# Two transformer blocks on one core: the moving columns of the main products in another order

## The reference

```
# block 1
z = rmsnorm(x) @ w_in                       # 2048 -> 5200
... pooling mixer, top-k attention ...
x = x + concat(y_pool, y_attn) @ w_out      # 2048 -> 2048
up = rmsnorm(x) @ w_up                      # 2048 -> 11264
x = x + (silu(conv(gate)) * conv(val)) @ w_down    # 5632 -> 2048
# block 2
proj = rmsnorm(h) @ w_in_2                  # 2048 -> 8000
... two attentions; w_uq_2, w_ukv_2, w_branch_a_2, w_branch_b_2 ...
h = h + mixed @ w_out_2                     # 2048 -> 2048
h = h + (silu(hn @ w_gate_2) * (hn @ w_up_2)) @ w_down_2   # 2048 -> 2 x 5632 -> 2048
return rmsnorm(h)
```

## Time and profile before

| | |
|---|---|
| median of 3 executions | 2428.22 us (2427.38 to 2428.86) |
| the profiled execution: time | 2428.58 us |
| its span, first to last instruction | 2426.7 us |
| PE busy | 2417.1 us, 11684 matmuls |
| PEld busy | 2036.5 us, 11684 loads |
| DVE, ACT, POOL busy | 1371.2, 1178.5, 59.8 us |
| transfers | 449.40 MB, mean 185 GB/s |
| granted TensorE clock, mean | 0.999 |

### The profile page before, as it was taken

The page is one execution under the profiler, slowest core; times in us unless marked ns, Lnnn a source line. Parts: engine busy times, 40 slices in busy tenths (PEclk is TensorE's granted clock), DMA queues, the critical chain, the costliest instruction groups (busy, mean ns, idle before and its releaser), DMA issues.

```text
span 2426.7 us, 31051 instructions
## 1 busy us (share of the span) xinstructions
PE 2417.1 (100%) x11684; PEld 2036.5 (84%) x11684; DVE 1371.2 (57%) x1594; ACT 1178.5 (49%) x1534; POOL 59.8 (2%) x100
## 2 busy tenths in 40 slices
PE   9999999999999999999999999999999999999998
PEld 8788888888888888888888888888888888888887
DVE  5675456777777765445454454665545445454544
ACT  5544445555555544445455544544444444444443
POOL 0000000000000000001120000000000000000000
PEclk9999999999999999999999999999999999999999
DMA  7665456666666655556655556556666666666664
GB/s 249 176 178 167 148 183 182 192 186 185 192 192 179 195 196 190 190 190 186 186 165 174 162 160 184 189 184 189 187 189 188 190 190 189 189 190 207 193 193 155
DMA packets 241049, 449.40 MB, mean 185 GB/s; under 512 B 20100, under 2 KB 26980, under 8 KB 240832
## 3 DMA queue, kind: packets, MB, share of 16 engines
q1 hardware_dynamic: 239952, 445.57, 60.4%
q0 software_dynamic: 624, 2.24, 0.3%
q10 hardware_dynamic: 384, 0.37, 0.0%
HBM read 446.02 MB, written 2.10 MB: 185 GB/s over the span
## 4 chain that ended last, share of the span: by engine, by line
PE 99%; issue 0%; DMA 0%; DVE 0%; ACT 0%; POOLq 0%; POOL 0%; ACTq 0%; DVEq 0%
PE acc L576 25%; PE acc L578 25%; PE acc L577 25%; PE acc L925 7%; PE bank L925 7%; PE bank L928 3%; PE acc L928 3%; PE bank L567 2%; PE bank L749 1%; PE bank L777 0%; PE bank L807 0%; PE bank L726 0%; PE bank L778 0%; PE bank L752 0%; DMA stage<-in_gains 0%
## 5 line engine op out<-in xcount | busy, mean ns | idle before, releaser
L1350 DVE TENSOR_TENSOR w_lo<-w_raw,w_hi 128x1024 fp32r<-128x1024 f32 (+1 forms) x843 | 1027.6, 1221 | 1019.4 <-ACT w_hi L1015 1018.7
L1015 ACT ACTIVATE w_hi<-w_raw 128x1024 fp32r<-128x1024 f32 (+1 forms) x843 | 887.2, 1055 | 1110.9 <-PE acc L578 985.8
L576 PE MATMUL acc<-w_hi,xT 128*128 128x512 f32 (+1 forms) x1532 | 603.4, 394 | 0.0
L578 PE MATMUL acc<-w_hi,xT 128*128 128x512 f32 (+1 forms) x1532 | 595.1, 388 | 0.0
L577 PE MATMUL acc<-w_lo,xT 128*128 128x512 f32 (+1 forms) x1532 | 594.2, 388 | 0.0
L578 PEld LDWEIGHTS acc<-w_hi,xT 128*128 128x128 f32 x1532 | 287.7, 188 | 59.6
L576 PEld LDWEIGHTS acc<-w_hi,xT 128*128 128x128 f32 x1532 | 287.9, 188 | 57.9 <-issue 1.3
L577 PEld LDWEIGHTS acc<-w_lo,xT 128*128 128x128 f32 x1532 | 288.1, 188 | 56.4
L576 PE MATMUL acc<-w_hi,f_hi 128*128 128x512 f32 x688 | 268.3, 390 | 0.0
L578 PE MATMUL acc<-w_hi,f_lo 128*128 128x512 f32 x688 | 267.9, 389 | 0.0
L577 PE MATMUL acc<-w_lo,f_hi 128*128 128x512 f32 x688 | 267.9, 389 | 0.0
(11 more groups left out here) (235 smaller groups left out, 1812.9 us busy)
## 6 DMA issues: line engine op xcount, KB each, us to landing
w_raw<-in_w_up SPq DMA_DIRECT2D x264, 512.0 KB, 3.7
w_raw<-in_w_in SPq DMA_DIRECT2D x199, 512.0 KB, 3.6
w_raw<-in_w_down SPq DMA_DIRECT2D x176, 512.0 KB, 4.2
w_raw<-in_w_gate SPq DMA_DIRECT2D x88, 512.0 KB, 3.6
w_raw<-in_w_out SPq DMA_DIRECT2D x64, 512.0 KB, 3.6
w_raw<-in_w_branch_a SPq DMA_DIRECT2D x16, 512.0 KB, 3.7
w_raw<-in_w_branch_b SPq DMA_DIRECT2D x16, 512.0 KB, 3.8
w_raw<-in_w_in SPq DMA_DIRECT2D x10, 320.0 KB, 3.1
```

The costliest lines, as they stand in the source:

```text
L576: pe.matmul(o, l, w_hi[:, slot, k, 0:width], start=start, stop=False)
L578: last = pe.matmul(o, m, w_hi[:, slot, k, 0:width], start=False, stop=stop)
L1015: act.activation(in_slot(w_hi, slot, width), in_slot(w_raw, slot, width), ACT.Copy).then_inc(w_split_hi, 1)
L1350: dve.tensor_tensor(in_slot(w_lo, slot, width), in_slot(w_raw, slot, width), in_slot(w_hi, slot, width).bitcast(F32), ALU.subtract).then_i ...
```

## The change

A view `swept` is put around the moving operand and the PSUM output of the three products in `columns` and in `last_columns`. A row of 512 columns is seen as 2 halves of 16 pieces of 16 columns. The order becomes: piece 15 of the lower half, piece 15 of the upper half, piece 14 of the lower half, and so on down to piece 0 of the upper half; inside a piece the columns ascend. A row of 320 columns becomes 2 halves of 10 pieces. The output is written in the same order, so that each column lands where it landed before. The number of instructions, their operands' contents, the sums and all waits stay as they are.

```diff
+            def swept(v):
+
+                return v.rearrange("p (h x e) -> p x h e", h=2, e=16)[:, ::-1]
+
             def columns(c, k, width, operand, start, stop, g):
...
-                    o = acc[g][t][:, 0:width]
+                    o = swept(acc[g][t][:, 0:width])
                     l, m = hi[:, t * P:(t + 1) * P], lo[:, t * P:(t + 1) * P]
-                    pe.matmul(o, l, w_hi[:, slot, k, 0:width], start=start, stop=False)
-                    pe.matmul(o, l, w_lo[:, slot, k, 0:width], start=False, stop=False)
-                    last = pe.matmul(o, m, w_hi[:, slot, k, 0:width], start=False, stop=stop)
+                    h, r = swept(w_hi[:, slot, k, 0:width]), swept(w_lo[:, slot, k, 0:width])
+                    pe.matmul(o, l, h, start=start, stop=False)
+                    pe.matmul(o, l, r, start=False, stop=False)
+                    last = pe.matmul(o, m, h, start=False, stop=stop)
...
-                    pe.matmul(acc[par][t][:], h, w_hi[:, slot, k], start=False, stop=False)
-                    pe.matmul(acc[par][t][:], h, w_lo[:, slot, k], start=False, stop=False)
-                    last = pe.matmul(acc[par][t][:], l, w_hi[:, slot, k], start=False, stop=ends and k == KC - 1)
+                    o, w, r = (swept(v) for v in (acc[par][t][:], w_hi[:, slot, k], w_lo[:, slot, k]))
+                    pe.matmul(o, h, w, start=False, stop=False)
+                    pe.matmul(o, h, r, start=False, stop=False)
+                    last = pe.matmul(o, l, w, start=False, stop=ends and k == KC - 1)
```

## The result

The changed kernel takes 2474.92 us (median; 2474.58 to 2475.47) against 2428.2, a ratio of 1.0193 with a 95% interval of 1.018 to 1.0206: 46.7 us slower. The forecast was no change, 2428, with a range up to 2445; the time lies 30 us above that range.

A forecast was written before the change was run, and what follows sets the result against it. PE's matmuls were taken to bound the kernel, 99% of the span. 2426.7 us of span + 0 + 0 + 0, with 1.9 us around it, gave 2428.6 profiled, 2428.2 as median; likeliest 2428, range 2336 to 2445.

The forecast's parts named there:

- What bounds the kernel, and how many products are touched: PE's matmuls are 99% of the span; 7884 touched products of 512 columns and 96 of 320, 7.9 us per nanosecond.
- first part: 31 jumps within each matmul's moving operand: taken as 0, at most a lost column period per piece, 13.3 ns or +105 us.
- the jumps cost: Rival, slower: one lost column period at each piece of a touched matmul, +105 us, 2533 us; slower cases together 0.24.
- its own mark: If jumps cost, a fixed amount per piece: 320 columns (20 pieces) grow by 5/8 of what 512 grow by.
- second part: The changed order of PSUM addresses, each column touched again after 512 columns as before: taken as 0.
- The rival that ran to 4111 us: Non-contiguous PSUM output makes each column take two periods, +1683 us; chance 0.04 at the much slower end.
- third part: Order in which the moving operand meets the next weight load: taken as 0, possible -11.1 to +11.1 ns, 87.5 us either way.
- My mark for this part: If the loss to the weight loads changes, 512 and 320 columns shift by the same nanoseconds, the load being the same.
- The faster rival: Loss to weight loads depends on the order: all of it gone gives 2340.7 us, half 2384; chance 0.34.
- the 13.3 ns rest: Part of each 226.7 ns touched matmul beyond streaming 512 columns, read as the load taking fetches from the stream.

The follow-up runs named there:

- e3: Changed kernel with pieces of 16 from alternating halves taken from the lower end up (alternate up), both operands alike: 2529.8 us, ratio 1.0421.
- e14: Changed kernel with xT, f, y, m all moved by 64 bytes against w_hi and w_lo: 2427.3 us, ratio 0.9996 to the kernel before.
- e2: Changed kernel with the moving operand ascending again, only the PSUM output in the new order: 2428.1 us, ratio 1.0001 to the kernel before.
- e13: Kernel before, ascending, with f, y, m and the latents moved 64 bytes on by a filler: 2450.1 us, ratio 1.0091.
- e6: Kernel before with orders and stationary columns loaded varied by group: ascending 230.0, 230.0, 231.7 ns with 96, 64, 32 columns, against 226.7 with 128.
- e15: Kernel before, ascending, with a 64-byte filler ahead of w_hi, moving w_hi, w_lo, f, y, m together and leaving xT: 2436.5 us, ratio 1.0036.
- e1: Changed kernel with the PSUM output ascending again, only the moving operand in the new order: 2475.3 us, ratio 1.0194 to the kernel before.
- e7: Inner tensors moved 64 bytes by a filler, four orders by group, all else ascending as before: ascending 233.4 ns, alternate halves down 226.8 ns.
- e5: Kernel before with sixteen orders, one per group of four matrices: alternate halves up 250.0 ns with pieces of 4 columns, 240.0 with 16, 226.8 with 64.
- e10: Kernel before with fewer moving columns per matmul, several orders by group: at 256 columns 120 ns ascending and alternate up, 117.8 single run down, 120.8 alternate down.
- e16: Kernel before with only the up projection's 256-column products in four other orders: 2429.46 us in one execution, those products at 117.8 to 120.8 ns.
- e9: Kernel before with only the stationary tile's start moved by columns, several orders by group: ascending 233.3 ns at 48 bytes, 226.7 at 256.
- e12: Changed kernel with f, y, m and the latents moved 64 bytes on by a filler, xT left in place: 2461.9 us, ratio 1.0138 to the kernel before.
- e17: Kernel before, ascending, with w_lo alone moved by 64 bytes, f, y, m kept in place: 2462.7 us, ratio 1.0141.
- e4: Changed kernel with pieces of 16 in a single run down over all 512 columns, no alternation: 2477.4 us, ratio 1.0203 to the kernel before.
- e11: Kernel before with other orders, stationary steps and starts by group: single run down in pieces of 1 233.4 ns, every second stationary column ascending 233.4 ns.

## Why the prediction was wrong, point by point

**What bounds the kernel, and how many products are touched: right.** PE holds 99% of the chain in both kernels, and a nanosecond on each touched product was worth about what I said: the 13.3 ns of e3 came to 101.9 us, 7.6 us for one against the 7.9 forecast.

**The jumps (first part, 0 with a bound of +105 us): 0 was right for this order.** In e14 the products of f and m have 31 jumps each and the pace of before. My reason, that unbroken rows keep the pace, didn't show it, and for the alternate order upward, at 240.0 ns at each place tried, it stays open whether jumps as such cost. The rival "the jumps cost" had the right sign for the wrong reason; its own mark, 320 columns growing by 5/8 of 512, is absent (146.8 ns).

**PSUM (second part, 0): right**, shown by e2 (1.0001). The rival that ran to 4111 us has no ground here.

**The order in which the moving operand meets the next weight load (third part): this is the step that failed.** I took 0 because many pairs of tiles all showed one pace, and noted that all of them start at multiples of 512 bytes from one another. That second remark was the decisive one. The one pace came from the common low bits of the addresses, and e13 shows what a shift of 64 bytes does to it (+6.67 ns). The uniform pace was thus no evidence that order is free. The term measured +6.67 ns for a product of 512 columns in most undisturbed stretches, 46.1 us in the span, where the sum has 0. That is within the +11.1 ns and +87.5 us that I had put as the upper bound of this part. The range should have reached to that bound, 2516 us, but stopped at 2445; I had given 0.15 to the stretch above it in which the result fell. My mark for this part, the same number of nanoseconds at 512 and 320 columns, was wrong too: 320 columns didn't move.

**The faster rival** stood on the same mechanism and on reading the 13.3 ns rest as fetches lost to the load. e6 refutes that reading for 512 columns: fewer loaded columns didn't lower the distance. The comparison of 80 with 128 stationary columns in the earlier trace rows, 116.2 against 119.3 ns, didn't show it either, since e15 has 113.5 ns with all 128. For 512 columns no order or place tried had a mean under 226.7 ns. Only the 256-column products went under their old pace.

**What was shown and what stays open.** Shown: the cost is on the moving side and not in PSUM (e1, e2); for the ascending order and the changed one it depends on the relative start address of stationary tile and moving row (e7, e13, e14, e15); the number of jumps alone doesn't set it (e5, e14), and a shorter load doesn't lower it (e6); at the old place it vanishes with pieces of 256 bytes and more (e5) and is 2 ns or less either way with 256 columns (e10, e16); more than one pace can hold for the same kind of products (e9, e12, and the 230.0 ns in the changed kernel); neighbours matter (e17). Open: why alternate up costs 13.3 ns at every place tried, and what makes a stretch settle at one pace or another. That weight load and moving stream compete for something in the fetch, in a rhythm set by both addresses, would account for the trading of places, but it is argued, not shown. The independent read ports of the Trainium skill's page "TensorE: Matmul & The Clock Gate" (Part 2: What happens when you issue a matmul) would give no such dependence, and what the two share no run here can show.

## What to carry to other kernels

A uniform pace over many tiles is no proof that the order of addresses is free, if all tiles share their alignment: look for what they have in common before taking a sensitivity as zero. With fp32r products and a load for each, a filler of 64 bytes or a reordered row can move every matmul of 512 columns by 6.67 ns (3%) or more, so an access order and a placement are to be tested together, and an unrelated tensor put ahead of the operands can bring the same loss. Jumps in pieces of 256 bytes or more, at the place of before, and the new order of the PSUM output cost nothing here.

## What the runs showed of the hardware that was not expected

- The mean distances between products of 512 fp32r columns lay mostly at 226.7, 233.3 and 240.0 ns, 544, 560 and 576 periods of 2.4 GHz, with 230.0, 236.7, 243.3 and 250.0 beside them, and some in between (228.9, 232.4, 235.5). The same mean can be an even pace (e4: 233 and 234 ns) or turns of 236 and 231 ns (the changed kernel).
- A fully reversed row, in pieces of one column on both sides (e11), costs 6.7 ns and no more.
- Products of the same matrix, with the same order and placement, ran at 236.7 ns in one stretch and at 226.7 ns in another of one execution (e12), and changed over at an interruption.
- A smaller stationary load made ascending products slower: 226.7 ns with 128 columns, 231.7 with 32 (e6).
- 256-column products went from 119.8 to 113.5 ns by a filler of 64 bytes between `xT` and the weights (e15).
